# Memory and forget attention run in eight rounds among the panels of the next head, and GpSimd takes the low parts

## The reference, cut to what matters

```python
u = rmsnorm(h, mix_norm)
fq, fk, fv, ff, dq, dk, dv, iq, ik, iw, mq, g = split(u @ w_in)
o_a = fox_attention(rmsnorm(fq), rmsnorm(fk), fv, log_sigmoid(ff + b))   # 8 heads of 64, causal, forget sums
o_b = dsa_attention(rope(rmsnorm(dq)), rope(rmsnorm(dk)), dv, rope(iq), rope(ik), iw)  # top 128 keys by an indexer
km, vm = split(rmsnorm(mem) @ w_mem_kv)
o_c = memory_attention(rmsnorm(mq), rmsnorm(km), vm)                      # 4 heads of 128, 256 keys
h = h + sum(sigmoid(g) * (stack(o_a, o_b, o_c) @ w_branch)) @ w_out
```

## Time and profile before

| | |
|---|---|
| runs | 2229.23, 2231.22, 2225.75 us |
| profiled execution: its time, its span | 2231.07 us, 2229.1 us |
| mean granted clock of PE | 0.956 |
| busy share PE, weight loads, Vector, ACT, GpSimd | 91%, 74%, 51%, 22%, 52% |
| chain that ended last | PE 78%, Vector 15%, ACT 3% |

### The profile page before, as it was taken

How to read it: one execution, slowest core, us unless ns; L and a number is a source line. 1 busy time by engine, 2 the same in 40 slices (tenths; PEclk the granted TensorE clock), 3 DMA queues, 4 the chain that set the end, 5 groups by cost and what they waited for, 6 DMA issues and landing times.

```text
span 2229.1 us, 25757 instructions
## 1 busy us (share of the span) xinstructions
PE 2028.2 (91%) x8955; PEld 1639.3 (74%) x8955; DVE 1127.0 (51%) x1388; ACT 492.0 (22%) x896; POOL 1156.0 (52%) x672
## 2 busy tenths in 40 slices
PE   7999999778689889888999999998898869999996
PEld 6888887466477678776778888886676648888884
DVE  5334510565676637876664433009868685333104
ACT  3111100322233432243121111002266421111001
POOL 4666666254142245502666666655454456666661
PEclk9999999889799999989999999999999979999998
DMA  4333223222021113300333333333200012333330
GB/s 146 95 96 101 94 94 86 67 76 67 20 66 38 38 48 85 94 1 29 95 90 99 94 94 99 99 94 85 66 1 1 19 57 85 96 101 94 94 94 38
DMA packets 259800, 163.73 MB, mean 73 GB/s; under 512 B 30380, under 2 KB 249582, under 8 KB 259614
## 3 DMA queue, kind: packets, MB, share of 16 engines
q1 hardware_dynamic: 258080, 157.90, 24.5%
q10 hardware_dynamic: 1662, 5.06, 0.7%
HBM read 160.81 MB, written 2.13 MB: 73 GB/s over the span
## 4 chain that ended last, share of the span: by engine, by line
PE 78%; DVE 15%; ACT 3%; issue 2%; POOL 1%; DMA 0%; ACTq 0%; POOLq 0%; DVEq 0%; SPq 0%
PE bank L658 16%; PE bank L659 16%; PE bank L660 16%; PE bank L726 5%; PE bank L727 5%; PE bank L725 5%; DVE work L1729 3%; PE bank L787 2%; PE bank L1045 1%; PE bank L1047 1%; PE bank L1046 1%; DVE rowmax L1690 1%; DVE work L1659 1%; PE bank L830 1%; DVE u_lo L1608 1%
## 5 line engine op out<-in xcount | busy, mean ns | idle before, releaser
L586 POOL TENSOR_SCALAR w_hi<-raw 128x1024 fp32r<-128x1024 f32 x298 | 322.8, 1083 | 923.3 <-PE bank L660 647.6
L588 POOL TENSOR_TENSOR w_lo<-raw,w_hi 128x1024 fp32r<-128x1024 f32 x298 | 746.5, 2505 | 24.9
L658 PE MATMUL bank<-u_hi,w_hi 128*128 128x512 f32 x1568 | 639.3, 408 | 34.0 <-DVE u_lo L1608 18.3
L659 PE MATMUL bank<-u_lo,w_hi 128*128 128x512 f32 x1568 | 617.8, 394 | 0.0
L660 PE MATMUL bank<-u_hi,w_lo 128*128 128x512 f32 x1568 | 617.3, 394 | 0.0
L658 PEld LDWEIGHTS bank<-u_hi,w_hi 128*128 128x128 f32 x1568 | 298.6, 190 | 117.9 <-issue 31.5
L659 PEld LDWEIGHTS bank<-u_lo,w_hi 128*128 128x128 f32 x1568 | 299.3, 191 | 69.4 <-issue 10.1
L660 PEld LDWEIGHTS bank<-u_hi,w_lo 128*128 128x128 f32 x1568 | 298.6, 190 | 63.5
L1634 DVE TENSOR_TENSOR work<-bank,work 128x512 f32<-128x512 f32 x66 | 45.6, 691 | 285.1 <-PE bank L660 285.1
L725 PE MATMUL bank<-hid_hi,w_hi 128*128 (+1 forms) x480 | 186.7, 389 | 0.0
L726 PE MATMUL bank<-hid_lo,w_hi 128*128 (+1 forms) x480 | 186.7, 389 | 0.0
(11 more groups left out here) (442 smaller groups left out, 2826.6 us busy)
## 6 DMA issues: line engine op xcount, KB each, us to landing
raw<-in_w_in SPq DMA_DIRECT2D x52, 512.0 KB, 3.7
raw<-in_ffn_w_gate SPq DMA_DIRECT2D x44, 512.0 KB, 3.8
raw<-in_ffn_w_up SPq DMA_DIRECT2D x44, 512.0 KB, 3.7
raw<-in_ffn_w_down SPq DMA_DIRECT2D x44, 512.0 KB, 3.4
raw<-in_w_gate SPq DMA_DIRECT2D x22, 512.0 KB, 3.7
raw<-in_w_up SPq DMA_DIRECT2D x22, 512.0 KB, 3.8
raw<-in_w_down SPq DMA_DIRECT2D x22, 512.0 KB, 3.5
raw<-in_w_branch SPq DMA_DIRECT2D x12, 512.0 KB, 3.4
```

The costliest lines, as they stand in the source:

```text
L586: pool.tensor_scalar(w_hi[:, s, :], raw[:, k, :], 1.0, 1.0, ALU.mult, ALU.mult).then_inc(hi_done, 1)
L588: pool.tensor_tensor(w_lo[:, s, :], raw[:, k, :], w_hi[:, s, :].bitcast(F32), ALU.subtract).then_inc(split_ready, 1)
L658: pe.matmul(outs[:, 0:n], wh, rhs_hi[:, c, :], start=(c == 0), stop=False)
L659: pe.matmul(outs[:, 0:n], wh, rhs_lo[:, c, :], start=False, stop=False)
```

## The change

The memory and forget stages become eight **rounds**, four for a memory head each and four for a pair of forget heads each, written out without loops. A round runs one attention and, among its matmuls, chunk by chunk, the panels of the next head or pair: on PE the panels are Python generators (`mem_panels`, `fox_panels`) that stop before each chunk, and `go_on(panels, n)` lets n chunks through. The last memory round runs the panels of forget pair 0; the last forget round runs the first four of the 24 gate panels, whose raw sums ACT copies to `sig` and passes through the sigmoid later. Gate panels 4 to 7 then hold all 24 index scores, six a panel from chunk 2 on.

The attention has fewer banks: one for scores (0), two for transposed scores (2, 3), 6 for the outputs of memory heads, with 7 for their denominators, 6 and 7 for forget heads. Panels use 4 (q, v) and 5 (k and the other), and bank 1 (AUX) is shared by the rotation, both head sums and the transposed values. k's raw copy goes to a tile of its own, `k_raw`; v's raw copy goes to W[1] after q's low part. Low parts of memory, forget and sparse attention (8 + 32 + 32 instructions) move from Vector to GpSimd, in a fixed order among the splits. `fst2` is cleared by GpSimd (eight memsets of 128 x 512), its ones are written by Vector in forget round 0. ACT issues four loads of forget sums a round. The rotations of dq in the top-k stage come half a panel earlier on PE (n = 11, 15, 19, 23, before chunk 4). The functions of an attention that were inside `attend` are returned by `attention`; `attend` keeps the order of the sparse attention and of the second block.

The diff's core. The first `fox_slot` is PE's, the second ACT's, the third Vector's; the same holds for the two `fox_tasks` (ACT, Vector). Memory's counterparts are alike, without rotation, with `ones` for `blk64`.

```diff
-        mst2, m_end = lay("m2_", s_at, MEM_TILES)
-        assert m_end <= s_at + 8192
+        mst2, m_end = lay("m2_", o_at, MEM_TILES)
+        assert m_end <= o_at + 8192
+        k_raw = at("k_raw", [P, S], x_at + 22528)
...
+        MEM_BANKS, FOX_BANKS = ((0,), (2, 3), (6,), 7), ((0,), (2, 3), (6, 7), None)
+        AUX, Q_BANK, K_BANK = 1, 4, 5
+        USUAL = S_BANKS, T_BANKS, O_BANKS, DEN_BANK
+        DQ_SUMS, DQ_TURNS = (9, 13, 17, 21), (11, 15, 19, 23)
...
+            def forget_rows():
+                pool.wait_ge(a_o, A_FOX[3])
+                pool.wait_ge(split_ready, U_FOX + 6)
+                for e in range(2):
+                    for n in ("qh", "ql", "kh", "kl"):
+                        last = pool.memset(fst2[f"{n[0]}{e}{n[1]}"][:].bitcast(F32), 0.0)
+                last.then_inc(c_two, 1)
...
+            def mem_and_fox():
+                for u in range(U_MEM, U_MEM + 6):
+                    one(u)
+                steps = steps_of(mem_heads)
+                for i in range(4):
+                    u = U_MEM + 4 * (i + 1)
+                    one(u + 2)
+                    low_part(A_MEM, mem_heads, steps[2 * i])
+                    low_part(A_MEM, mem_heads, steps[2 * i + 1])
+                    for k in (3, 4, 5):
+                        one(u + k)
+                steps = steps_of(fox_heads)
+                for p in range(4):
+                    u = U_FOX + 4 * (p + 1)
+                    if p == 0:
+                        forget_rows()
+                    low_part(A_FOX, fox_heads, steps[8 * p])
+                    one(u + 2)
+                    for k in (1, 2, 3):
+                        low_part(A_FOX, fox_heads, steps[8 * p + k])
+                    one(u + 3)
+                    for k in (4, 5):
+                        low_part(A_FOX, fox_heads, steps[8 * p + k])
+                    one(u + 4)
+                    for k in (6, 7):
+                        low_part(A_FOX, fox_heads, steps[8 * p + k])
+                    one(u + 5)
...
+            mem_and_fox()
+            for u in range(U_GATE + 6, U_BR + SPL):
+                one(u)
+            low_parts(A_DSA, dsa_heads)
+            run(U_BR + SPL, U_B2)
...
+            def fox_panels(p):
+                u, h = U_FOX + 4 * p, H_FOX + 2 * p
+                pe.wait_ge(v_raw, VR_FOX + p)
+                for c in chunks(u, Q_BANK, *U):
+                    if c == 1:
+                        pe.wait_ge(r_raw, RR_MEM + 4)
+                        pe.wait_ge(s_lo, S_FOX + 3 * p)
+                        rotate(AUX, iq[:, p, :])
+                    yield
+                pe.wait_ge(r_raw, RR_FOX + p)
+                for c in chunks(u + 1, K_BANK, *U):
+                    if c == 3:
+                        pe.wait_ge(r_out, R_IQ + p + 1)
+                        head_sum(h, AUX, W[0], blk64)
+                    yield
+                pe.wait_ge(h_raw, h + 1)
+                for c in chunks(u + 2, Q_BANK, *U):
+                    if c == 2:
+                        pe.wait_ge(h_std, h + 1)
+                        head_sum(h + 1, AUX, W[2], blk64)
+                    yield
+                pe.wait_ge(h_raw, h + 2)
+                for c in chunks(u + 3, K_BANK, *U):
+                    if c == 3:
+                        pe.wait_ge(h_std, h + 2)
+                        values(VR_FOX + p, AUX, W[1])
...
+            def mem_slot(i):
+                scores, scores_t, values_mm = attention(A_MEM, mem_heads, MEM_BANKS)
+                steps = steps_of(mem_heads)[2 * i:2 * i + 2]
+                panels = mem_panels(i + 1) if i < 3 else fox_panels(0)
+                for qt in range(TT):
+                    scores(i, qt)
+                    go_on(panels, 1)
+                go_on(panels, 4)
+                for h, k, kb, t, b in steps:
+                    scores_t(h, k, kb, t)
+                    go_on(panels, 2)
+                go_on(panels, 4)
+                for h, k, kb, t, b in steps:
+                    values_mm(h, k, kb, b)
+                    go_on(panels, 4)
+                for _ in panels:
+                    pass
...
+            def fox_slot(p):
...
+                for qt in range(TT):
+                    scores(2 * p, qt)
+                    go_on(panels, 1)
+                for qt in range(2):
+                    scores(2 * p + 1, qt)
+                    go_on(panels, 1)
+                for k in range(2):
+                    t_of(k)
+                    go_on(panels, 1)
+                    scores(2 * p + 1, 2 + k)
+                    go_on(panels, 1)
+                for k in (2, 3):
+                    t_of(k)
+                    go_on(panels, 2)
                 for k in range(4):
+                    v_of(k)
+                    go_on(panels, 1)
+                go_on(panels, 1)
+                for k in range(4, 8):
+                    t_of(k)
+                    go_on(panels, 2)
+                for k in range(4, 8):
+                    v_of(k)
+                    go_on(panels, 1)
+                for _ in panels:
+                    pass
...
+                        if n in DQ_TURNS and c == 4:
+                            j = DQ_TURNS.index(n)
+                            pe.wait_ge(h_out, H_DQ + j + 1)
+                            pe.wait_ge(r_out, R_DQ + j)
+                            rotate(7, dq[:, j, :])
...
+            def fox_tasks(p):
+                u, h, st = U_FOX + 4 * p, H_FOX + 2 * p, (fst, fst2)[p % 2]
+                def q_square():
+                    act.wait_ge(s_lo, S_FOX + 3 * p)
+                    head_square(h, u, Q_BANK, W[0], W[1])
+                def k_square():
+                    act.wait_ge(r_out, R_IQ + p + 1)
+                    head_square(h + 1, u + 1, K_BANK, W[2], k_raw)
+                def stds():
+                    head_std(h, AUX, W[0], HD)
+                    head_std(h + 1, AUX, W[2], HD)
+                def q_high():
+                    act.wait_ge(h_out, h + 1)
+                    halves_high((st["q0h"], st["q1h"]), W[1], s_hi)
+                def v_copy():
+                    act.wait_ge(s_lo, S_FOX + 3 * p + 1)
+                    value_copy(u + 2, Q_BANK, W[1])
+                def k_high():
+                    act.wait_ge(h_out, h + 2)
+                    halves_high((st["k0h"], st["k1h"]), k_raw, s_hi)
...
+            def forget_sums(p):
+                st = (fst, fst2)[p % 2]
+                act.wait_ge((c_one, c_two)[p % 2], 2)
+                if p >= 2:
+                    act.wait_ge(a_o, A_FOX[3] + 2 * p - 2)
+                for e in range(2):
+                    r = HALVES[1 - e].start
+                    sums = c_dram[:, 2 * p + e, :]
+                    act.dma_start(st[f"q{e}h"][r:r + 2, :].bitcast(F32), sums).then_inc(ld_c, 16)
+                    act.dma_start(st[f"k{e}h"][r + 2:r + 4, :].bitcast(F32), sums).then_inc(ld_c, 16)
...
+            def fox_slot(p):
...
+                exps(*steps[0])
+                exps(*steps[1])
+                if p < 3:
+                    q_square()
+                else:
+                    gate_copy(0)
+                exps(*steps[2])
+                exps(*steps[3])
+                if p < 3:
+                    forget_sums(p + 1)
+                    k_square()
+                    stds()
+                    load_exp()
+                    q_high()
+                else:
+                    gate_copy(1)
+                output(2 * p)
+                exps(*steps[4])
+                exps(*steps[5])
+                if p < 3:
+                    v_copy()
+                    k_high()
+                exps(*steps[6])
+                if p == 3:
+                    gate_copy(2)
+                exps(*steps[7])
+                if p < 3:
+                    v_high()
+                output(2 * p + 1)
+                if p < 3:
+                    other()
...
+            def fox_tasks(p):
+                h, s, st = H_FOX + 2 * p, S_FOX + 3 * p, (fst, fst2)[p % 2]
+                q = iq[:, p, :]
+                dve.wait_ge(h_out, h)
+                rope(R_IQ + p, q, AUX, cos1[:], sin1[:], W[2], q)
+                head_norm(h, W[0], W[1], G_FQ)
+                halves_low(s, (st["q0l"], st["q1l"]), W[1], (st["q0h"], st["q1h"]))
+                head_norm(h + 1, W[2], k_raw, G_FK)
+                halves_low(s + 1, (st["k0l"], st["k1l"]), k_raw, (st["k0h"], st["k1h"]))
+                value_low(s + 2, st, AUX)
...
+            def fox_slot(p):
+                maxes, diagonal, output = attention(A_FOX, fox_heads, lambda r, g: oT[r, g, :], FOX_BANKS)
+                for h in (2 * p, 2 * p + 1):
+                    for qt in range(TT):
+                        maxes(h, qt)
+                    diagonal(h)
+                if p == 0:
+                    attention(A_MEM, mem_heads, lambda r, g: oT[r, 8 + g, :], MEM_BANKS)[2](3)
+                    value_ones(fst2)
+                    dve.wait_ge(c_two, 1)
```

(14 more changed lines are left out.)

503 lines of the change are left out of this document (271 added, 232 removed).

## The result

The changed kernel takes **2226.59 us** (median of 19 runs, 2222.51 to 2230.77), the kernel before 2231.38 in the same session (19 runs): a ratio of 0.9979, 95% interval 0.9972 to 0.9987. That is 4.8 us or 0.21% less: clear of zero by its interval, but smaller than the 0.3% that I had called distinguishable from no change. The forecast was 2210.5 us, 18.7 us less. The profiled execution shows 6.0 us less span, at the same share of PE.

What follows compares the result with a forecast made beforehand. PE, busy 91% of the span, was taken as the bound, leaving only idle or slow-clock time. Stretch 3.7, gate panels -21.7, index hole 2.3, sparse attention -3: -18.7; 2231.07 - 18.7 - 1.8 = 2210.5 us, range 2186 to 2230.

Steps and rivals of the forecast that it cites:

- diagonal 0.9: Vector's diagonal (shift products) in a forget round, before the rotation PE waits for: put at 0.9 us of 9.0.
- Memory rounds: Memory rounds 0 to 2, walked through PE, ACT and Vector's chain: 27 us each with some contention, 81 for three.
- Memory round 3: Last memory round, carrying forget panels 0: 38.9 us, with a 4.5 us hole waiting for k's low halves.
- Forget rounds: Forget rounds 0 to 2: 54.8, 50 and 50 us, including a PE stop on the rotation and slow clock.
- Step (a): Forget round's start: last score issued at 10.3 us, PE at the rotation stop 3.1 later, then standing 5.9.
- (b): Forget round after the rotation stop: head sum and 5.4 us of work to the end of k, 6.3 in the sum.
- (c): Forget round after k: ACT and Vector chain of 11.1 us against 7.3 of PE work, so 3.8 more.
- (d): Forget round's end: ten chunks, two short blocks, four value blocks and the transposes, 10.4 us.
- Index and top-k: Stages behind the rounds: four gate panels fewer, -21.7 us; index hole grows by 2.3; top-k 0.
- Rival A: Short waits in the rounds: no clock fall, less contention, k's lows in time; stretch 320, time 2192 us; chance 0.22.
- Rival C: Slower: GpSimd's splits and low parts delay Vector's two-input ops in the rounds, 28 us more, 2238; chance 0.10.
- Rival B: Comes to nothing: seven rounds each 2 to 3 us longer than walked, within 6.7 of 2229; chance 0.14.

Runs made afterwards that it cites:

- experiment 6: Changed kernel with GpSimd making memory's two low parts ahead of the split of panel u+2, not behind it; 2219.84 us.
- experiment 12: Changed kernel with GpSimd's split of panel u+4 waiting, from memory round 0 on, until Vector has written q's low part; 2231.55 us.
- 11: experiment 7 with experiment 6's idea replaced: memory's low parts on Vector, GpSimd only splitting there, and the rotation early in memory round 3; 2189.75 us.
- Experiment 3: Changed kernel with GpSimd's split of panel u+2 and following low parts waiting, in forget rounds, for the second head's shifts; 2219.91 us.
- experiment 4: Changed kernel with the sparse attention's 32 low parts back on Vector; 2230.72 us.
- experiment 2: Changed kernel with Vector rotating the next iq between the second and third row maxima of the pair's second head, in forget rounds; 2195.12 us.
- experiment 7: experiment 2's kernel with ACT issuing the next forget rows' loads behind the first head's output, not ahead of k's square; 2192.66 us.
- experiment 5: Changed kernel with memory's value panel copied early into the unused half of k_raw, not into W1 behind q's low part; 2236.49 us.
- experiment 8: experiment 7 plus the edits of experiment 5 and experiment 6, early rotation in memory round 3, and ACT's exponentials moved ahead in forget rounds; 2213.35 us.

## Why the prediction was wrong

The direction was right; the size was a quarter of the forecast. The step that failed is the length of Vector's operations in its chain: I took them as they are with GpSimd idle (diagonal 0.9, low part of q 0.7), and beside GpSimd's splits they took 3.76 and 2.09. By the steps of the prediction:

- *First panels, 28:* 28.8. *Memory rounds, 27 each:* 28.4, 29.5, 27.9. The term at fault is the chain of Vector, "reciprocal 3.35 and product 0.85 ... high and low part": I had the low part of q at about 0.7 and it is 2.09, so PE waited 1.9 before the transposes, not 1.1. "With some contention" had left 1 us for it and for the clock, which fell in rounds 0 and 1 (0.96, 0.92; 1.7 us of busy PE between rounds 1 and 2). Experiments 6 and 12, which change only GpSimd's order, bring the low part to 0.7; in 11, where its splits come earlier again, it is back at 2.09.
- *Memory round 3, 38.9 with a 4.5 us hole:* 36.5 with 2.24. k1's low part took 1.43 us, not 2.77: it lay beside w_hi, which GpSimd ends sooner, and not beside w_lo.
- *Forget rounds, 54.8, 50, 50:* 56.7, 54.0, 54.2; this is the larger half of the error, 10.1 us. Step (a) was 1.3 too short: up to the stop PE stands nowhere longer than 0.5 us, and it gets there after 14.7 us, where I had counted 10.3 + 3.1. Then **"diagonal 0.9"**: it is 3.76, and the stop is 7.8 and not 5.9 (10.7 for 8.6 in round 0). Experiment 3 takes the 2.9 us from the diagonal by moving GpSimd alone, and the stop falls to 5.9. The 1.3 us of step (a) are a count of mine and no experiment bears on them. Steps (b), 6.3 and the clock's 3, and (c), 11.1, measured 9.4 and 10.9; (d) was 0.8 short.
- *Forget round 3, 36:* 37.2. *Index and top-k, -19.4:* -19.8, with the hole at 6.3 for 7.1. *Sparse attention, -3:* -4.5, confirmed by experiment 4.

The stretch is thus 14.4 us longer than walked, the rest 1.7 better. What I had right is what mattered for a remedy: the place, cause and releaser of the stop on the rotation, in every forget round, with the slow clock behind it. What I did not do was ask whether it had to be there. Rival A's remark, that the stop "is in program order", was read as a bound; moving three of Vector's operations was worth 31.5 us (experiment 2), and 33.9 with ACT's loads moved as well (experiment 7).

Rival C had the mechanism, GpSimd in Vector's way, and was dismissed with "q's lows show 0.69 now, splits being over". That was a wrong reading of the kernel before. Its trace shows a split there:

```profile
494.06 0.69 DVE L1678 TENSOR_TENSOR m_ql<-work,m_qh 128x512 fp32r<-128x512 f32 x1 [3.11 <-ACT m_qh L1179]
494.67 2.56 DVE L1678 TENSOR_TENSOR m_kl<-work,m_kh 128x256 fp32r<-128x256 f32 x1
...
494.19 2.76 POOL L588 TENSOR_TENSOR w_lo<-raw,w_hi 128x1024 fp32r<-128x1024 f32 x1
```

The low part of q starts 0.13 us ahead of w_lo and keeps its 0.69; the low part of k behind it, half as wide, takes 2.56 us, in all four heads (0.42 without a split). So the old schedule already paid the price, on the operation behind, and a look at m_kl would have shown it. In the new one PE ends a panel, and so releases a split, at other points of Vector's chain. Nor is the price a matter of 1 us on every two-input op: one or two operations of a chain are hit, one of them by up to 2.1 us. Rival B's outcome came about (within 6.7 us of 2229), in good part for C's reason: the longer stops in the forget rounds and the low part of q in the memory rounds make some 10 of the stretch's 14.4 us. Rounds of 54 stood in the text as the sign that I would be too low.

## What to carry to other kernels

Where several engines' orders are written out by hand, look for the wait that is only order: the rotation had its input before, and stood behind a division that nobody waited for yet. Once it was out of the way, the 3.77 us of the shift products cost nothing that PE waited for. A stop that is slack may be holding something else back: taking it away (experiment 5) let GpSimd run onto the critical operation and cost 10 us. Two edits whose effects are known one by one can make a new wait together (experiment 8). And cost a moved queue on another engine by what it will lie beside in the new schedule, not by the durations in the old.

## What the runs showed of the hardware

**Some Vector operations wait until GpSimd's instruction is over.** In memory round 3 of the changed kernel three products of the rotation lie beside one split:

```profile
572.21 0.98 DVE L1918 TENSOR_TENSOR iq<-iq,cos 128x512 f32<-128x512 f32 x1
573.11 0.68 DVE L1922 TENSOR_TENSOR work<-bank,sin 128x512 f32<-128x512 f32 x1
573.89 2.08 DVE L1925 TENSOR_TENSOR iq<-iq,work 128x512 f32<-128x512 f32 x1
...
572.74 2.69 POOL L597 TENSOR_TENSOR w_lo<-raw,w_hi 128x1024 fp32r<-128x1024 f32 x1
```

The one that reads PSUM takes its 0.68 us in the midst of w_lo; the next, with both inputs in SBUF, ends 0.5 us behind w_lo's end at 575.43. The first is hit by w_hi, which runs from 571.58 to 572.65: it starts within it and ends 0.5 us behind it, and so does k1's low part at 597.93 (1.43 us, w_hi from 597.36 to 598.82). So both instructions of a split do it. In memory round 0 w_lo ends at 500.80 and the low part of q at 501.35; in experiment 5, 507.11 and 507.39; in experiment 12, 503.77 and 504.05. An operation that starts first (experiment 6, by 0.3 us) keeps its time, and then w_lo is longer: 2.71 there, and 2.91 in memory round 0, where the product of q starts just ahead of it, for 2.39. Reciprocals beside GpSimd's instructions stay at 3.35, and row maxima, which read PSUM, at 0.42 (256 columns) and 0.56 (384). The shift products, whose only full-width input is a constant in SBUF, are hit. By the Trainium skill (SBUF — State Buffer, "SBUF: two separate sides") the port pair that the two engines share is an exclusive lock, held for a whole instruction by whichever starts first, and not a split of bandwidth; the traces here agree, to within 0.6 us. I had cited the page that says only that they contend. The price of a collision is therefore what is left of the other's instruction, at most 2.4 us for a w_lo here, and a position of 0.1 to 0.3 us decides who pays it.

**The clock's fall is not a function of the hole alone.** Stops of 7.8 and of 4.4 us were both followed by 1.2 GHz for 5 to 6 us (half of it lost), and holes of 0.6 to 2 us in some rounds and not in others: the 2.24 us hole before the first forget scores was followed by a clock of 1.00 over 600 to 607 us in the changed kernel, and in experiment 12, the same hole, by

```profile
603.00:610.00 7.00, 6.80 (x18) 4.70 (x19) 1.85 (x5) 0.00 (x0) 4.95 (x9) 0.59 0.28 75
```
